# Attention by kinds with half the key and value buffers, merge rows in shared rooms, and thirteen expert slots instead of ten

## What is computed

```
proj = rmsnorm(x) @ w_in              # FoX q|k|v|forget, SB q|k|v, two gates of 1024
y_fox = softmax(q.k/8 + C[t] - C[s]) @ v           # 8 heads of 64, C = cumulated log forget
y_sb  = exp(log_sigmoid(z) + tail(log_sigmoid(-z))) @ v   # 8 heads of 64, stick breaking
h = x + (sig(ga) * (y_fox @ w_o_fox) + sig(gb) * (y_sb @ w_o_sb)) @ w_out
# PEER: 8 heads, top 16 of 128 on each of two key halves, then top 16 of the 256 sums
act = gelu(expert_u[eidx] . n2);  out = h + sum(softmax(sc) * act * expert_v[eidx])
```

## Time and profile before

| | us |
|---|---|
| runs: median of 3 (lowest to highest) | 4281.25 (4277.36 to 4287.47) |
| the profiled execution's own time | 4279.13 |
| its span | 4277.3 |
| wave 0: project, attend, merge | 17 to 261, to 376, to 601 |
| wave 1 | 601 to 832, to 1129, to 1491 |
| wave 2 | 1491 to 1732, to 2053, to 2413 |
| wave 3 | 2413 to 2657, to 3028, to 3395 |
| wave 4 (attend, merge), then the last lots | 3395 to 3657, to 3930, to 4277 |

### The profile page before, as it was taken

The page is one execution under the profiler, slowest core; times in us unless marked ns, Lnnn a source line. Parts: engine busy times, 40 slices in busy tenths (PEclk is TensorE's granted clock), DMA queues, the critical chain, the costliest instruction groups (busy, mean ns, idle before and its releaser), DMA issues.

```text
span 4277.3 us, 32195 instructions
## 1 busy us (share of the span) xinstructions
PE 3242.6 (76%) x9738; PEld 1679.2 (39%) x9738; DVE 2864.9 (67%) x5568; ACT 1216.8 (28%) x2591; POOL 1389.5 (32%) x1086
## 2 busy tenths in 40 slices
PE   8989838588868595798876785899876677868665
PEld 3345623244435242455453332555453233334222
DVE  2012477587678975688579775788679766557865
ACT  1132112255311121566111121666211245111110
POOL 0000013243433333343333232334333233434553
PEclk9966969687879798788888897888888777888787
DMA  4413439899999889799999798787998788999997
GB/s 138 134 53 120 141 139 415 335 380 400 391 370 386 322 328 414 279 383 374 390 392 360 278 400 345 298 348 307 384 391 328 277 316 324 408 420 385 385 420 321
DMA packets 306602, 1388.17 MB, mean 325 GB/s; under 512 B 36384, under 2 KB 96960, under 8 KB 159968
## 3 DMA queue, kind: packets, MB, share of 16 engines
q0 software_dynamic: 154464, 1116.02, 64.7%
q1 hardware_dynamic: 121056, 243.75, 15.9%
q10 hardware_dynamic: 30912, 26.35, 1.9%
HBM read 1350.49 MB, written 35.10 MB: 324 GB/s over the span
## 4 chain that ended last, share of the span: by engine, by line
PE 35%; DVE 28%; DMA 18%; ACT 7%; issue 6%; SPq 5%; POOL 1%; ACTq 0%; DVEq 0%; POOLq 0%
DVE uv L1346 11%; PE pb L946 9%; DMA uv<-expert_uv,rows_u 8%; PE pv L777 7%; SPq L526 5%; DMA arena<-w_main 5%; PE pb L887 3%; PE pb L860 3%; PE pb L730 3%; PE pb L759 2%; PE pb L835 2%; DVE held L1369 2%; DMA arena<-w_stream 2%; PE pv L946 2%; DVE arena L1407 1%
## 5 line engine op out<-in xcount | busy, mean ns | idle before, releaser
L680 POOL DMA_INDIRECT uv<-expert_uv,rows_u x1024 | 1334.8, 1304 | 2250.8 <-PE pv L777 1168.8
L777 PE MATMUL pv<-uv,diag 128*128 128x512 f32 x2316 | 1244.7, 694 | 377.4 <-ACT diag L1083 336.9
L1346 DVE CUSTOM_DVE_ANT_0 uv<-uv,nr 128x1024 f32<-128x1024 f32 x1056 | 1241.5, 1220 | 204.8 <-DMA uv<-expert_uv,rows_u 171.0
L777 PEld LDWEIGHTS pv<-uv,diag 128*128 128x128 f32 x2316 | 504.0, 226 | 1024.7 <-issue 982.4
L946 PE MATMUL pb<-arena 128*128 128x512 f32 x1280 | 620.9, 643 | 163.2 <-DMA arena<-w_main 163.1
L1369 DVE SCALAR_TENSOR_TENSOR held<-uv,wgt,held 128x1024 f32<-128x1024 f32 x477 | 613.0, 1285 | 16.9 <-DVE wgt L1357 0.3
L1090 ACT ACTIVATE gel<-dots 128x4 f32<-128x4 f32 x264 | 54.2, 205 | 1792.2 <-DVE dots L1346 1712.5
L946 PEld LDWEIGHTS pb<-arena 128*128 128x128 f32 x1280 | 258.9, 207 | 497.0 <-issue 316.9
L730 PE MATMUL pb<-arena 64*128 64x512 f32 (+6 forms) x544 | 281.2, 635 | 125.2 <-DVE arena L1328 43.0
L759 PE MATMUL pb<-arena 128*128 128x64 f32 (+3 forms) x1728 | 256.2, 297 | 40.3 <-ACT o L1072 40.3
L759 PEld LDWEIGHTS pb<-arena 128*128 128x128 f32 (+3 forms) x1728 | 237.1, 202 | 106.6 <-issue 68.5
(11 more groups left out here) (147 smaller groups left out, 2670.5 us busy)
## 6 DMA issues: line engine op xcount, KB each, us to landing
arena<-w_main SPq DMA_DIRECT2D x80, 1024.0 KB
arena<-w_stream SPq DMA_DIRECT2D x80, 1024.0 KB
uv<-expert_uv,rows_u POOLq DMA_INDIRECT x1024
arena<-x SPq DMA_DIRECT2D x16, 512.0 KB, 19.6
scratch_gates<-arena ACTq DMA_DIRECT2D x32, 256.0 KB, 11.3
arena<-scratch_gates SPq DMA_DIRECT2D x8, 1024.0 KB, 21.7
arena<-scratch_c_p SPq DMA_DIRECT2D x8, 520.0 KB
arena<-x_t SPq DMA_DIRECT2D x8, 512.0 KB
```

Of the source, the lines that this page charges most:

```text
L680: pool.indirect_dma_start(out=uv[k % NU][:].rearrange("p a n -> p (a n)"), out_offset=None, in_=io["expert_uv"][:, :], in_offset=bass.Indi ...
L777: mm = nc.tensor.matmul(pv[:, c * BANK:(c + 1) * BANK], diag[n % ND][:], uv[k % NU][:, 1, c * BANK:(c + 1) * BANK], start=n == first, stop ...
L1346: nc.vector.tensor_tensor_reduce(out=u, in0=u, in1=row[:], scale=1.0, scalar=0.0, op0=ALU.mult, op1=ALU.add, accum_out=dots[b % 2][:, k % ...
```

## The change

1. NU goes from 10 to 13: three more slots of 1 MB.
2. `Plan` lists a head pair's units kind by kind: four units of kind 0 (two heads, two tiles), then four of kind 1; in wave 4 two and two. What was a pair is now a pair and a kind: `pairs` has twice the entries, each with four DMAs (six for the samples) and its own set.
3. There are two sets of one kind where there were two of both kinds, so half the room; in wave 4, where queries are narrow, three sets. `load_pair(i)` waits for the last unit of entry i - 2 (i - 3 in wave 4). The load inside project at column block 7 is of kind 0 alone; the one of kind 1 comes at the start of attend, behind the two rows of C.
4. The rows of C have two buffers for three; the probability buffers are one ring of four for both kinds, the softmax statistics a ring of four.
5. In merge the rows of x share the rooms of the attention outputs `o`, so their load waits until the outputs have been transposed (`o_turned`); `g_row` lies in a gate room and is loaded once all rows are merged; `rest`, `qh` and the small tables lie in the gate rooms too. No instruction of merge is added or taken away.
6. ARENA shrinks from 22640 to 16480 floats, which pays for the three slots.

The shares of the lots and their places among the steps stay.

```
-NU = 10
+NU = 13
...
-                    for hh in range(2):
-                        for t in sub:
-                            for k in range(KINDS):
+                    for k in range(KINDS):
+                        for hh in range(2):
+                            for t in sub:
...
-        for i, (g, sub, hp) in enumerate(self.pairs):
-            total[i % 2] += 16 * (12 if sub[0] == SAMPLES else 8)
+        for i, (g, sub, hp, k) in enumerate(self.pairs):
+            b = (i - self.first_pair[g]) % (3 if sub[0] == SAMPLES else 2)
+            total[b] += 16 * (6 if sub[0] == SAMPLES else 4)
...
                 def load_pair(i):
-                    g, sub, hp = plan.pairs[i]
-                    if i >= 2:
-                        sp.wait_ge(summed_up, plan.pair_last[i - 2] + 1)
+                    g, sub, hp, k = plan.pairs[i]
+                    sets = 3 if sub[0] == SAMPLES else 2
+                    if i >= sets:
+                        sp.wait_ge(summed_up, plan.pair_last[i - sets] + 1)
...
                 def load_ck(i):
-                    if i >= 3:
-                        sp.wait_ge(minimum, plan.kind_no[plan.ck_last[i - 3]] + 1)
+                    if i >= 2:
+                        sp.wait_ge(minimum, plan.kind_no[plan.ck_last[i - 2]] + 1)
...
                                 load_pair(i)
-                            load_ck(2 * i)
-                            load_ck(2 * i + 1)
+                            if pair[3] == 0:
+                                load_ck(i)
+                                load_ck(i + 1)
...
+                    sp.wait_ge(o_turned, tiles[-1] + 1)
                     for ti, t in enumerate(tiles):
                         sp.dma_start(xh[ti][0:r], io["x"][...]).then_inc(x_in[ti], 16)
-                    sp.dma_start(g_row, io["norm_ffn"].partition_broadcast(P)).then_inc(g_in, 16)
                     for c in range(NW, 8 + NW):
+                        if c == NW + 4:
+                            sp.wait_ge(merged, 2 * (tiles[-1] + 1))
+                            sp.dma_start(g_row, io["norm_ffn"].partition_broadcast(P)).then_inc(g_in, 16)
                         load_chunk(g, c)
...
                     if k == 0:
-                        if i >= 2:
-                            dve.wait_ge(turned, plan.turns[plan.unit_of[0, i - 2]][-1][0] + 1)
+                        if n >= 4:
+                            dve.wait_ge(turned, plan.turns[n - 4][-1][0] + 1)
```

More of the change, by code:

```diff
@@ L12 @@
 from contextlib import ExitStack
+from dataclasses import dataclass
 import concourse.bass as bass
@@ L58 @@
 CW = 4 * BANK
-ARENA = 22640
+ARENA = 16480
 def rows_of(t):
@@ L124 @@
              "samples": 1}
+@dataclass
+class AttentionRoom:
+    kt: list
+    vt: list
+    qt: list
+    ck: list
+    prob: list
+    low: list
+    probt: list
 class Projections:
@@ L203, in __init__ @@
         self.kind_no = [kinds[:n].count(kinds[n]) for n in range(len(kinds))]
-        self.unit_of = {(k, self.kind_no[n]): n for n, k in enumerate(kinds)}
         self.pieces, self.taken = [], []
@@ L305, in stream @@
         skt = sb("skt", [P, 2, NK])
-        o = [[sb(f"o{k}{i}", [P, WID]) for i in range(2)] for k in range(KINDS)]
+        o_rows = [sb(f"o{i}", [P, KINDS, WID]) for i in range(2)]
+        o = [[o_rows[i][:, k, :] for i in range(2)] for k in range(KINDS)]
+        xh = [o_rows[i][:].rearrange("p k n -> p (k n)") for i in range(2)]
         rows_pk = sb("rows_pk", [P, NK // 4], U32)
@@ L353, in stream @@
         mt = carve(KD, 2 * P)
[L354 to L358, removed]
         top = [carve(2, HEADS, TOPK) for _ in range(2)]
@@ L362, in stream @@
         sc, ex, ci = carve(HEADS, TOPK), carve(HEADS, TOPK), carve(HEADS, TOPK).bitcast(U32)
+        g_row = gate[1][:, 1, :]
+        rest = [gate[0][:, 0, i * BANK:(i + 1) * BANK].rearrange("p (j n) -> p j n", j=4) for i in range(2)]
+        qh = [gate[0][:, 1, i * BANK:(i + 1) * BANK].rearrange("p (a q) -> p a q", a=2) for i in range(2)]
+        n2t = ot
+        hit = gate[0].rearrange("p k (h n) -> p (k h) n", h=HEADS // 2).rearrange("p h (a b) -> p h a b", a=TOPK)
+        cand = gate[1].rearrange("p k (h n) -> p (k h) n", h=HEADS // 2)
+        rest2 = mt
+        at[0] = gates_at + KINDS * D
         cab, caf = carve(2, HEADS, TOPK).bitcast(U32), carve(2, HEADS, TOPK)
@@ L371, in stream @@
         sq = carve(BANK)
-        tst_more = [carve(BANK) for _ in range(2)]
+        tst = [carve(BANK) for _ in range(2)]
         ss, rstd = carve(ABREAST), carve(ABREAST)
@@ L413, in stream @@
         sk_in = sem("sk_in")
-        pair_in = [sem(f"pair_in{i}") for i in range(2)]
-        ck_in = [sem(f"ck_in{i}") for i in range(3)]
+        pair_in = [sem(f"pair_in{i}") for i in range(3)]
+        ck_in = [sem(f"ck_in{i}") for i in range(2)]
         scored = sem("scored")
@@ L522, in load_pair @@
[L522 to L539, removed]
@@ L722, in scores @@
                     diag_at = w - r
-                    half = slice(hh * DH, (hh + 1) * DH)
-                    pe.wait_ge(pair_in[pair % 2], plan.pair_loaded[pair])
+                    half, b = slice(hh * DH, (hh + 1) * DH), plan.pair_set[pair]
+                    pe.wait_ge(pair_in[b], plan.pair_loaded[pair])
                     for m, c0, c1 in plan.pieces[n]:
@@ L729, in scores @@
                         masked = c1 > diag_at
-                        mm = nc.tensor.matmul(pb[0:r, m % 3, 0:c1 - c0], qt[k][pair % 2][half, tj * P:tj * P + r],
-                                              kt[k][pair % 2][half, c0:c1], start=True, stop=not masked)
+                        mm = nc.tensor.matmul(pb[0:r, m % 3, 0:c1 - c0], room(t).qt[b][half, tj * P:tj * P + r],
+                                              room(t).kt[b][half, c0:c1], start=True, stop=not masked)
                         if masked:
@@ L1025, in magnitudes @@
                         return
+                    if n >= 4:
+                        act.wait_ge(turned, plan.turns[n - 4][-1][0] + 1)
                     if i >= 2:
-                        before = plan.unit_of[1, i - 2]
-                        act.wait_ge(turned, plan.turns[before][-1][0] + 1)
                         act.wait_ge(exponent, i - 1)
-                    z, mag = prob[1][i % 2], low[i % 2]
+                    z, mag = room(t).prob[n % 4], room(t).low[i % 2]
                     for m, c0, c1 in plan.pieces[n]:
@@ L1052, in turn_out @@
                     r = query_rows(plan.units[n][5])
+                    probt = room(plan.units[n][5]).probt
                     if n >= 2:
```

101 lines of the change are left out of this document (58 added, 43 removed).

## The result

The changed kernel takes 4345.99 us (median of 4 runs, 4344.68 to 4349.37), the kernel before 4283.69 in the same session. The ratio is 1.0148, with a 95% interval of 1.0133 to 1.0163: **slower by 1.5%**. Forecast were 4245 us with a range of 4155 to 4350, and slower had a chance of 0.30.

A forecast was written before the change was run, and what follows sets the result against it. No engine was full; the bound shifted between DMA engines (wave 1's attend, mid-project, the last stretch) and TensorE (wave 3's attend). Terms -51 - 58 - 20 + 95 = -34 against 4279 gave 4245 us, range 4155 to 4350.

The forecast's parts named there:

- What bounds the kernel: Whole kernel: no engine is full; wave 1's attend is near the DMA engines' limit, wave 3's near TensorE's.
- Term 1: End of project, waves 1 to 3: half load lets the last w_main chunk come earlier, 17 us a wave, -51 us.
- Term 2: Three more slots: gains in projects, attends and from wave 4's merge to the end, -58 us.
- The three refills at the start of the projects: Start of three projects: three more slots give idle DMA engines 7.7 us of gathers each, 23 us gained.
- Term 3: Wave 4's attend: half loads with three sets shorten TensorE's waits and the wait for C's row, -20 us.
- Term 4: Attend, waves 1 to 3: loads released only one step ahead come late, TensorE waits at scores, +95 us.
- the 14 us for runs of one kind: Wave 3's attend: four runs of kind 1 leave TensorE idle, 3.5 us each, 14 us.
- Costed at nothing: Moved loads of x and g_row in merge, and two buffers for C: no cost; wave 0 up to 5 us either way.
- Rival 1: Attend, waves 1 to 3: late keys win, all TensorE waits on the path, +80 us, 4359 us; slower, chance 0.30.
- Its clock part: TensorE after 18 waits for late keys: slower clock costs two us each, 36 us more.
- Rival 2: Key loads: thirteen slots make a half load 1.3 times as long, 4348 us; some 0.04 of the 0.30 for slower.

The follow-up runs named there:

- e4: Changed kernel, thirteen slots, but q, k and C rows are released by the last scores, v by summed values, with its own semaphore; 4176.4 us, ratio 0.9761.
- e1: Changed kernel without the three extra slots (NU = 10), nothing else; 4369.5 us, ratio 1.0201 to the kernel before.
- e2: Kernel before with only the units' order changed to kind by kind, still two whole sets and ten slots; 4273.9 us, ratio 0.9981.
- e6: e4 with the pair loaded inside project issued one column block later, behind the last chunk of w_main; 4161.7 us, ratio 0.9717.
- e7: e4 with no pair loaded inside project, the first entry loaded at the start of attend; 4168.4 us, ratio 0.9738.
- e5: e4 with ten slots (NU = 10) instead of thirteen; 4218.4 us, ratio 0.9848 to the kernel before.
- e8: e4 with q and k released by summed values, as late as in the changed kernel; only the semaphores are separate; 4192.7 us, ratio 0.9790.

## Why the prediction was wrong

By its own steps, against the phases:

- **What bounds the kernel: right.** Wave 1's attend near the DMA engines' limit, wave 3's near TensorE's; in e4, with nothing late, the shares are 1.00 and 0.83.
- **Term 1, -51 us, failed.** The step was "the chunk is issued 20 us earlier", of which I took 17 as time won, with 10 as the lower bound. Counted from the start of project it was issued 24 to 27 us earlier and used 7.3, 1.5 and 1.5 us earlier, 10 us in all. In wave 1 it was in use 39 us after its issue, for 22 before. The window of the changed kernel from 781 to 803 us, in which TensorE waits for it, has a DMA share of 1.02:

```profile
781.00:803.00 22.00, 0.40 (x1) 0.00 (x0) 5.15 (x9) 0.00 (x0) 3.06 (x3) 0.61 1.02 419
```

  The DMA engines were full while it was waited for (in waves 2 and 3 the share is 0.93 and 0.94); an earlier place in SP's queue did not make them less so. What halving the pair was worth shows in e1, where the projects are 13 us shorter than before, with e2 showing that the order gives none of it (231.0, 240.4 and 243.7 us). e6 and e7 move the pair away and get 47 us of waits back, of which 16 and 11 reach the phases of project.
- **Term 2, -58 us: the mechanism held, one part did not.** Behind wave 4's attend I had 20 and it was 21 (24 and 23 between the pairs of runs that differ in slots alone); wave 1's attend had 10, and e5 to e4 shows 12, which late keys hid: from e1 to the changed kernel the three attends grew by 9. The three refills at the start of the projects had 23; slots alone gave 8 there with no load late (e5 to e4) and nothing with late ones (e1 to the changed kernel, +1.6). Term 1 and the refills together stood for 74 us and gave 12: **62 us of the miss**, which is 104 us by the profiled executions (+70 for -34) and 101 by the medians.
- **Term 3, -20 us, went the other way, +5.** Three sets of halves are released one step ahead too, and there are five such loads for two: with the same ten slots e1 has 288 us where the kernel before has 262. The wait for the row of C did shrink, from 19.3 to 14.8. Split release with ten slots (e5) takes 240 us, so the late loads of wave 4 cost 48 of e1's 288. Another 25 us of the miss.
- **Term 4, +95 us, was right in kind and nearly in size, partly by luck.** The attends grew by 107 us, and by 98 with ten slots (e1); the forecast with term 2's 15 us in them was 80, so 27 of the miss are here. The parts were off in ways that cancelled. Of the six loads a wave that I had as late only four were. Each took 15 to 27 us from release to scores where I had 19 for the load; the waits were 11 us in the mean and not 8. I took 81 of 149 us as lost; beside 133 us of waits the attends grew by 107. TensorE's idle time there rose from 48, 36 and 35 us to 76, 77 and 75, for waits of 51, 49 and 34: the idle time of before took in 23 us in wave 1, 7 in wave 2 and none in wave 3, 30 in all, where I had it take 68. Wave 0 and the merges, costed at nothing, gave 10 us back. And the 14 us for runs of one kind were nothing (e2). Its full price was hidden from this sum: 170 us by e4, as late keys also held up wave 4 and took back half of what the slots give.
- **Costed at nothing.** The moved loads of merge show no cost: the merges of waves 1 to 3 are 5 us shorter, and 8 with ten slots. The two buffers for C were not free: VectorE waits 9 us for them in wave 1.
- **Rival 1** named the outcome, and 4359 was 13 us off, but by luck: it has 163 us of waits where the attends grew by 107, 36 us for the clock, and terms 1 and 2 in full, 109 us less, most of which did not come. Its clock part is not seen as time: the granted clock fell to 0.78 and 0.79 in the attends of waves 1 and 2 from 0.82, but TensorE was busy for 251, 287 and 331 us in the three attends and for 249, 285 and 336 before. I gave it 0.30 because wave 4 had hidden half of each wait at VectorE; TensorE, the engine at 84 to 91%, was the one to ask. Rival 2 fell with e1, and the rule of the Trainium skill that I set beside it ("DMA: Bandwidth & Descriptors", "Queues, rings and completion order": turns between the queues) agrees with that run, 126 us of waits with ten slots and 133 with thirteen.

## What to carry to other kernels

Before halving a buffer, count the steps between the last reader of the old contents and the first of the new, in units of the pipeline, and compare that lead with how long the load takes while other queues run, not alone. Parts of a buffer with different last readers should be released one by one and be waited for by a semaphore of their own (e8: the semaphore was the larger part): here that brought back all of the lead with no memory, and made a change that cost 1.5% into one that gains 2.4%, or 2.8% with the project's load behind its last chunk. When a transfer is moved ahead in a queue whose engines are full, expect its wait to come back at the next transfer, and take only what the phase as a whole gets shorter.

## What the runs showed that I had not expected

- A load of q, k and v rows (0.7 to 1.2 MB, v in pieces of 512 B) took 15 to 27 us from release to use in waves 1 to 3 beside running gathers, while q and k alone came 10 to 12 us after release where TensorE waited for them at all (e8). In wave 0, without gathers, a smaller load of 0.4 MB has landed 3.4 us after its first issue (e1).
- The same wait for the last chunk of w_main, 15 to 31 us, stands in the kernel before, in the changed one, with ten slots and with thirteen, with a whole pair ahead of it and with half of one; only with none ahead does it fall to 5.6 to 5.9.
- TensorE's granted clock was 0.78 in wave 1's attend with four late loads and 0.83 in e4's without, yet TensorE's busy time there is 251 and 248 us.
